# Late heads: where VectorE's pair part and GpSimd's lookup of four PEER heads stand in a streaming-encoder layer

## What is computed

```python
h  = rms_norm(x, g_mix);  z = h @ w_in     # pool 512 | q 512 | k 128 | v 128 | gates 2 x 1024
x  = x + (sigmoid(gate_pool) * (pool_mixer(z_pool) @ w_branch_pool)
          + sigmoid(gate_attn) * (window_attention(q, k, v) @ w_branch_attn)) @ w_out
# PEER: 8 heads, 128 x 128 experts of one neuron, 16 of them per token and head
q  = (rms_norm(x, g_ffn) @ w_q).reshape(T, 8, 256)
s1 = q[..., :128] @ keys_1.T;  s2 = q[..., 128:] @ keys_2.T
v1, i1 = top_k(s1, 16);  v2, i2 = top_k(s2, 16)
vals, ci = top_k(v1[:, None] + v2[None, :], 16)            # over 16 x 16 pairs
e_idx = i1[ci // 16] * 128 + i2[ci % 16];  gates = softmax(vals)
y  = sum over the 128 chosen experts of gates * gelu(h . down[e]) * up[e]
out = rms_norm(x + y, g_final)
```

## Time and profile before

| | us |
|---|---|
| median of 3 runs | 3118.31 (3114.42 to 3119.14) |
| profiled execution, its own time | 3124.53 |
| its span | 3122.7 |
| busy: TensorE | 2829.1 (91%) |
| busy: VectorE | 2353.9 (75%) |
| busy: GpSimd | 2132.2 (68%) |
| busy: ScalarE | 928.8 (30%) |
| mixer, group 0: first xT2 transpose | 342.7 |
| mixer, group 1: first xT transpose | 467.9 |
| mixer, group 1: first branch product | 675.8 |
| gate table: first transpose | 1057.8 |

### The profile page before, as it was taken

How to read it: one execution, slowest core, us unless ns; L and a number is a source line. 1 busy time by engine, 2 the same in 40 slices (tenths; PEclk the granted TensorE clock), 3 DMA queues, 4 the chain that set the end, 5 groups by cost and what they waited for, 6 DMA issues and landing times.

```text
span 3122.7 us, 40081 instructions
## 1 busy us (share of the span) xinstructions
PE 2829.1 (91%) x15235; PEld 2474.5 (79%) x15235; DVE 2353.9 (75%) x4404; ACT 928.8 (30%) x1229; POOL 2132.2 (68%) x1553
## 2 busy tenths in 40 slices
PE   7999888599892399599999999999999999999996
PEld 6688767378781388589989998999899989998995
DVE  2322499532289699398998998889899888989898
ACT  4232432132430399222222222222222222222221
POOL 5334576724366698478877877788777878887774
PEclk9899998699996699799999999999999999999998
DMA  4022421112320188988899998999889989898986
GB/s 144 32 75 95 156 72 50 34 48 96 128 68 0 53 237 228 319 329 328 322 329 328 327 332 298 327 331 329 309 327 327 328 299 332 326 328 311 330 323 222
DMA packets 268048, 716.48 MB, mean 229 GB/s; under 512 B 20496, under 2 KB 106256, under 8 KB 267728
## 3 DMA queue, kind: packets, MB, share of 16 engines
q0 software_dynamic: 111152, 404.54, 34.8%
q1 hardware_dynamic: 156704, 309.38, 29.8%
HBM read 657.47 MB, written 56.36 MB: 229 GB/s over the span
## 4 chain that ended last, share of the span: by engine, by line
PE 41%; DVE 6%; DMA 5%; POOL 4%; issue 2%; ACT 1%; DVEq 0%; SPq 0%; ACTq 0%
PE abank L1427 7%; PE abank L1429 7%; PE abank L1428 7%; PE ybank L1443 7%; PE ybank L1444 7%; PE ybank L1445 7%; DMA up<-in_down,e_idx 3%; POOL up L1377 2%; DVE up L1565 2%; DVE acc L1580 2%; POOL tdown_lo L1382 1%; DMA up<-in_up,e_idx 1%; DVE y L1627 1%; DVE w L1616 1%; POOL tup_lo L1386 0%
## 5 line engine op out<-in xcount | busy, mean ns | idle before, releaser
L1427 PE MATMUL abank<-h2T_hi,tdown_hi 128*128 128x320 f32 x2048 | 635.0, 310 | 40.0 <-DVE h2T_lo L1631 30.7
L1429 PE MATMUL abank<-h2T_hi,tdown_lo 128*128 128x320 f32 x2048 | 635.5, 310 | 0.0
L1428 PE MATMUL abank<-h2T_lo,tdown_hi 128*128 128x320 f32 x2048 | 635.1, 310 | 0.0
L748 POOL TENSOR_TENSOR m_wlo<-m_raw,m_whi 128x1024 fp32r<-128x1024 f32 x116 | 280.3, 2421 | 412.9 <-ACT m_whi L573 411.2
L1580 DVE SCALAR_TENSOR_TENSOR acc<-up,e_act,acc 128x1024 f32<-128x1024 f32 x381 | 489.8, 1286 | 87.8 <-DMA up<-in_up,e_idx 70.3
L1565 DVE CUSTOM_DVE_ANT_0 up<-up,acc 128x1024 f32<-128x1024 f32 x384 | 458.8, 1216 | 109.7 <-DMA up<-in_down,e_idx 98.7
L1443 PE MATMUL ybank<-tup_hi,w_hi 128*128 128x512 f32 x1280 | 504.6, 394 | 19.1 <-DVE y L1627 17.8
L1444 PE MATMUL ybank<-tup_lo,w_hi 128*128 128x512 f32 x1280 | 503.6, 393 | 0.0
L1445 PE MATMUL ybank<-tup_hi,w_lo 128*128 128x512 f32 x1280 | 500.4, 391 | 0.0
L1377 POOL DMA_INDIRECT up<-in_down,e_idx x384 | 405.8, 1057 | 97.9 <-issue 82.1
L1377 POOL DMA_INDIRECT up<-in_up,e_idx x384 | 400.2, 1042 | 103.3 <-issue 89.5
(11 more groups left out here) (206 smaller groups left out, 4662.8 us busy)
## 6 DMA issues: line engine op xcount, KB each, us to landing
tdown<-in_downT SPq DMA_DIRECT2D x128, 512.0 KB
tup<-in_up SPq DMA_DIRECT2D x128, 512.0 KB
m_raw<-in_tiles SPq DMA_DIRECT2D x116, 512.0 KB, 3.3
all_table<-t_out SPq DMA_DIRECT2D x10, 4096.0 KB, 16.4
gates<-all_table SPq DMA_DIRECT2D x64, 640.0 KB
up<-in_down,e_idx POOLq DMA_INDIRECT x384
up<-in_up,e_idx POOLq DMA_INDIRECT x384
m_x<-in_x SPq DMA_DIRECT2D x8, 512.0 KB, 5.3
```

The source lines that it names most:

```text
L1427: nc.tensor.matmul(out, tdown_hi[:, q, at], h2T_hi[:, k, ts], start=k == 0, stop=False)
L1428: nc.tensor.matmul(out, tdown_hi[:, q, at], h2T_lo[:, k, ts], start=False, stop=False)
L1429: ins = nc.tensor.matmul(out, tdown_lo[:, q, at], h2T_hi[:, k, ts], start=False, stop=k == KD - 1)
```

## The change

Four heads of group 0 (4 to 7) are split. Their key part stays where it was and writes tiles of its own (vlate, ilate, in the space of g_ffn). Their pair part stands on VectorE behind m_lo of m = 1, 3, 5, 7 in group 1's merge, the softmax of group 0's gates behind the last of them, and ScalarE's Exp behind out3. GpSimd's lookup is called in halves i = 0, 1: for heads 4 to 6 one half per m from m = 2 on, between the low halves of ga and b of m + 1 (the second half of head 6 at m = 7, behind b7); head 7's behind the low halves of out2 and out5. `keep_choice(0)` goes behind pq2. The order of low halves and pool means in group 1 becomes that of group 0. In all sixteen heads the whole key part now comes before the pair sums, which one set of three instructions makes for all four tiles. The NDOT code goes. Cut to the core:

```diff
+LATE = {1: 4, 3: 5, 5: 6, 7: 7}
+FIRST_LATE = min(LATE.values())
...
-        vtop = place("vtop", [P, 2, 2, TOPK])
+        vtop = place("vtop", [P, TT, 2, TOPK])
-        cand = place("cand", [P, 2, NCAND])
-        cmask = place("cmask", [P, 2, NCAND])
+        cand = place("cand", [P, TT, NCAND])
+        cmask = place("cmask", [P, TT, NCAND])
...
+        vlate = [place(f"vlate{i}", [P, TT, 2, TOPK], F32, at_gffn + 512 * i) for i in range(4)]
+        ilate = [place(f"ilate{i}", [P, 2, TT, TOPK], U32, at_gffn + 2048 + 512 * i) for i in range(4)]
+        hits_late = [hits[0], place("hits_late", [P, TT * TOPK, TOPK], F32, at_pT)]
...
+            def gates_exp(g):
+                act.wait_ge(garg_ready, g + 1)
+                nc.scalar.activation(gate[:], gate[:], ACT.Exp).then_inc(gexp_ready, 1)
...
                 for j in range(4):
-                    if g and j == 1:
-                        act.wait_ge(garg_ready, g)
-                        nc.scalar.activation(gate[:], gate[:], ACT.Exp).then_inc(gexp_ready, 1)
                     keep_raw(g, 1 + j, "q", j)
...
                 for k in range(KD - 1):
                     after("out", k)
+                    if g and k == 3:
+                        gates_exp(g - 1)
...
-            def choose(g, hd):
+            def choose(g, hd, i):
...
-                for i in range(2):
-                    pool.wait_ge(hit_ready, g * 2 * PH + 2 * hd + i + 1)
+                of = hits if g + 1 == NG or hd < FIRST_LATE else hits_late
+                pool.wait_ge(hit_ready, g * 2 * PH + 2 * hd + i + 1)
...
+                if i == 0:
+                    return
...
+                through("q", 0)
                 pool.wait_ge(rope_in, 16 * (g + 1))
-                if g == 0:
...
+                pool_mean(g, 0)
+                through("q", 2)
+                pool_mean(g, 1)
+                through("gp", 0)
+                pool_mean(g, 2)
+                through("ga", 0)
+                pool_mean(g, 3)
                 through("b", 0)
                 for m in range(KD):
                     if 2 <= m + 1 < KD:
                         through("ga", m + 1)
-                    if g:
-                        gather_rows(dots_until(("merge", m - 1) if m else ("tile", 3, 1)) + TT)
+                    if g and m >= 2:
+                        choose(g - 1, FIRST_LATE + (m - 2) // 2, m % 2)
                     if m + 1 < KD:
                         through("b", m + 1)
...
+                if g:
+                    through("out", 2)
+                    choose(g - 1, PH - 1, 0)
+                    through("out", 5)
+                    choose(g - 1, PH - 1, 1)
                 through("pq", 2)
...
+                else:
+                    keep_choice(g - 1)
                 through("pq", 8)
-                for hd in range(PH):
-                    if hd < 3:
-                        tile_low(first + TILE["pq", 8] + 1 + 3 * hd)
-                    else:
-
-                        tile_low(first + NTILE + (3, 4, 7, 10, 10)[hd - 3])
-                    choose(g, hd)
+                for hd in range(PH if g + 1 == NG else FIRST_LATE):
+                    tile_low(first + min(NTILE + 3, TILE["pq", 8] + 1 + 3 * hd))
+                    for i in range(2):
+                        choose(g, hd, i)
...
+            def top_keys(g, hd, values, places):
+
+                dve.wait_ge(ss_ready, g * 2 * PH + 2 * hd + 2)
+                for ts in ((0, 1), (2, 3)):
+                    top16([(s12[hd // 2][:, hd % 2, i, t], smask[:, 2 * (t % 2) + i], values[:, t, i], places[:, i, t])
+                           for t in ts for i in range(2)])
+
+            def top_pairs(g, hd, values, places, to):
+
+                cols = slice(hd * TOPK, (hd + 1) * TOPK)
+                a, b = values[:, :, 0], values[:, :, 1]
+                last = NCAND - HALF_ROW
+                mark(nc.vector.tensor_tensor(cand[:, :, 0:TOPK], a[:, :, 0:1].to_broadcast([P, TT, TOPK]), b, ALU.add))
+                mark(nc.vector.tensor_tensor(
+                    cand[:, :, TOPK:last].rearrange("p t (i j) -> p t i j", j=HALF_ROW),
+                    a[:, :, 1:HALF_ROW].unsqueeze(3).to_broadcast([P, TT, HALF_ROW - 1, HALF_ROW]),
+                    b[:, :, 0:HALF_ROW].unsqueeze(2).to_broadcast([P, TT, HALF_ROW - 1, HALF_ROW]), ALU.add))
+                mark(nc.vector.tensor_tensor(cand[:, :, last:], a[:, :, HALF_ROW:],
+                                             b[:, :, 0:1].to_broadcast([P, TT, HALF_ROW]), ALU.add))
+                linked()
+                top16([(cand[:, t], cmask[:, t], gate[:, t, cols], ctop[:, t]) for t in range(TT)])
...
                     nc.vector.tensor_tensor(mlo[:, m], sg[:, m % 2, 0], mhi[:, m].bitcast(F32), ALU.subtract).then_inc(m_low, 1)
+                    if g and m in LATE:
+                        if m == min(LATE):
+                            dve.wait_ge(pooled_ready, (g + 1) * NPOOL)
+                        i = LATE[m] - FIRST_LATE
+                        top_pairs(g - 1, LATE[m], vlate[i], ilate[i], hits_late)
+                if g:
+                    gates_of(g - 1)
...
+                    if more and hd >= FIRST_LATE:
+                        top_keys(g, hd, vlate[hd - FIRST_LATE], ilate[hd - FIRST_LATE])
+                    else:
+                        top_keys(g, hd, vtop, itop)
+                        top_pairs(g, hd, vtop, itop, hits)
+            gates_of(NG - 1)
```

More of the change, by code:

```diff
@@ L70 @@
 EARLY = [("gp", 0), ("ga", 0), ("gp", 1), ("ga", 1)]
-NDOT = 0
-DOTS_AT = {("tile", 1, 0): 2, ("tile", 1, 1): 2, ("tile", 2, 0): 2, ("tile", 2, 1): 2, ("tile", 3, 0): 2,
-           ("tile", 3, 1): 2, ("merge", 0): 4, ("merge", 1): 4, ("merge", 2): 8, ("merge", 3): 8, ("merge", 4): 8,
-           ("merge", 5): 8, ("merge", 6): 8, ("merge", 7): 4}
-def dots_until(place):
-    places = list(DOTS_AT)
-    return min(NDOT, sum(DOTS_AT[q] for q in places[:places.index(place) + 1]))
+LATE = {1: 4, 3: 5, 5: 6, 7: 7}
+FIRST_LATE = min(LATE.values())
 def mixer_jobs():
@@ L144, in mixer @@
         wgrp = place("wgrp", [P, NPOOL, P])
+        at_gffn = here()
         gffn = place("gffn", [P, D])
@@ L155, in mixer @@
         hT = place("hT", [P, KD, TT, P], F32R)
+        at_pT = here()
         pT = place("pT", [P, NPOOL, PAD + TG])
@@ L352, in _ @@
                 for i in range(NTILE):
-                    if g and NDOT and i == TILE["out", 3]:
-                        sp.wait_ge(dot_done, NDOT)
-                        load_x(g)
                     if i == TILE["pq", 2]:
@@ L727, in _ @@
                     turned(g + 1, 0)
-            act.wait_ge(garg_ready, NG)
-            nc.scalar.activation(gate[:], gate[:], ACT.Exp).then_inc(gexp_ready, 1)
-            if NDOT:
-                act.wait_ge(dot_done, NDOT)
-                nc.scalar.activation(dots[:, 0:NDOT], dots[:, 0:NDOT], ACT.Gelu_apprx_tanh).then_inc(act_ready, 1)
+            gates_exp(NG - 1)
         @block.gpsimd
         def _(pool):
-            own, made, gathered = [0], [0], [0]
+            own, made = [0], [0]
             def link(ins):
@@ L878, in _ @@
         def _(dve):
-            own, dots_made = [0], [0]
+            own = [0]
             def link(ins):
@@ L914, in turned_low @@
                                                in1=hT[:, k].bitcast(F32), op0=ALU.mult, op1=ALU.subtract).then_inc(hT_low, 1)
-            def some_dots(g, *place):
-                to = dots_until(place) if g and place in DOTS_AT else 0
-                while dots_made[0] < to:
-                    c = dots_made[0]
-                    dve.wait_ge(down_in[c % TT], 16 * (c // TT + 1))
-                    if c == 0:
-                        dve.wait_ge(h2_in, 16)
-                    row = x[:, c % TT]
-                    nc.vector.tensor_tensor_reduce(out=row, in0=row, in1=gffn[:], scale=1.0, scalar=0.0, op0=ALU.mult,
-                                                   op1=ALU.add, accum_out=dots[:, c:c + 1]).then_inc(dot_done, 1)
-                    dots_made[0] += 1
+            between = []
@@ new lines, in top16, with step @@
+            def top16(chains):
+                def step(op, first):
+                    if between:
+                        between.pop(0)()
+                    for c, (scores, masked, values, places) in enumerate(chains):
+                        if not first:
+                            dve.wait_ge(dve_own, done[c])
+                        mark(op(scores, masked, values, places))
+                        done[c] = own[0]
+                done = [0] * len(chains)
+                step(lambda s, m, v, p: nc.vector.max(v[:, 0:8], s), True)
+                step(lambda s, m, v, p: nc.vector.match_replace(m, v[:, 0:8], s, NEG_BIG), False)
+                step(lambda s, m, v, p: nc.vector.max(v[:, 8:16], m), False)
+                step(lambda s, m, v, p: nc.vector.max_index(p[:, 0:8], v[:, 0:8], s), True)
```

(12 more changed lines are left out.)

195 lines of the change are left out of this document (54 added, 141 removed).

## The result

Nine executions each: before 3116.87 us (3114.39 to 3124.99), after **3099.57 us** (3094.11 to 3109.93). The ratio is 0.9944, interval 0.9936 to 0.9953: 17.3 us less, faster by 0.56%, a small gain but clear of the noise. The prediction was 3108, its range 3091 to 3118. The profiled execution after took 3103.28 us (span 3101.5), 21.2 us less than the profiled one before.

A forecast was written before the change was run, and what follows sets the result against it. VectorE's backlog on group 0's last heads was taken to delay group 1's front, and VectorE to bound the tail. Terms -39.5 + 23.7 + 8.7 - 3 = -10.1 us from the median 3118.3 gave 3108 us, range 3091 to 3118.

The forecast's parts named there:

- Front: Group 1 up to the merge: scores at 549.0 instead of 586.79, scores to merge 1.7 us shorter; -39.5 us.
- The template: Group 0's front without backlog: 46.22 us from last pool tile's copy to scores, 87.35 from there to first branch matmul.
- Cover of the front: Group 1's rope, first product wanted at 519.8: some 5 us of slack for VectorE, beyond which rope starts later.
- rope starting after 525: Group 1's front: named as a sign that the prediction is wrong.
- Rival 4: Front misses template as last four heads' keys outlast 519.8 by 6 us; 3114 us, within Rival 2's chance of 0.12.
- Merge: Group 1's merge: three pauses of 5.2 us before b3, b5, b7, each with 2.7 of lost clock; +23.7 us.
- Out tiles: Behind the merge: 0.9 us before out0, a pause of 5.1 before out3 and 2.7 of clock; +8.7 us.
- Tail: Group 1's heads: 2.4 us from three sums fewer per head, 0.5 from port waits; -3 us.
- Table to end: Stretch from the gate table to the end: no difference expected, 0 us.
- Rival 1: Merge pauses of 5.2 us come without clock loss and the out tiles fit in; 3091 us, chance 0.15.
- Rival 2: Port waits take the front's side gains, pq15's low half 2 to 4 us later, no tail gain; 3114 us, chance 0.12.
- Rival 3: Pair parts in the merge meet GpSimd's low halves, each of three pauses grows by 9.6 us; 3137 us, chance 0.08.

The follow-up runs named there:

- experiment i: On d, all eight heads of group 0 get their old form back; 3106.65 us, ratio 0.9962 to the kernel before.
- k: g with head 4's pair part and lookup back in place and the low halves of tensors k and v ahead of that lookup; 3067.95 us.
- c: Changed kernel with halves undone: whole lookups of heads 4 to 6 at m = 2, 4, 6, ahead of b(m+1)'s low half; 3120.86 us.
- h: Changed kernel, but group 1's pair sums are again two sets of three instructions over two tiles each, new order kept; 3100.07 us.
- e: Changed kernel with the old form of the heads back in group 1 alone; 3105.36 us.
- a: Changed kernel with VectorE's late pair parts ahead of the wait for m_hi and m_lo instead of behind m_lo; 3080.79 us.
- d: Changed kernel with no late head: pair parts and lookups of heads 4 to 7 back ahead of group 1's rope; 3104.97 us.
- g: a plus head 6's second lookup half behind out0's low half and head 7's first half behind out3's; 3069.81 us, ratio 0.9843 to before.
- b: Changed kernel with each lookup half in the merge behind b(m+1)'s low half instead of ahead, head 7's unmoved; 3080.01 us.

## Why the prediction was right, and where it was off

**The mechanism held.** The earlier scores, the pauses, their number and their cause came as forecast. The sum of the terms, -10.1, stands against -21.2 in the profiled executions and -17.3 in the medians; the 7 us by which the forecast gain was too small in the medians come mostly from the front.

**Front, -39.5 expected, -44.0 at b0.** The template was exact: from the last pool tile's copy to the scores 46.21 us (46.22 forecast), from there to b0 87.17 (87.35). The mis-sized step is its start: "Group 1's last pool tile is copied at 502.80" took that copy as fixed. It came 4.3 us earlier, 0.8 by a start that varies and 3.5 by the form of heads 4 to 7, as experiment i shows. The closer low halves, put at "about 1 us" and set against the port, gave 1.2, so that figure was right. What the sum left out is TensorE's clock behind them, 2.3 us: the old kernel ran the tiles there at 0.86, the new one at 1.00.

**Cover of the front.** "If this cover is gone, rope starts that much later; some 5 us of slack are left" was wrong in its size: k spent 13.9 us more and lost nothing that could be read. The sign "rope starting after 525" was wrong with it: in k rope starts at 526.76. Group 0's 60.84 tells when an unhindered VectorE did its first product, not when it was needed. Rival 4 was priced from the same number.

**Merge, +23.7 expected, +22.6 measured.** Hits 6.66 us behind the pair part's start (6.8), lookup 1.31 behind them (1.3), its first half 7.05 long (6.4), pause 5.45 (5.2), three times; clock 2.1 for each (2.7). The second halves cost nothing, as said; c shows what they would have cost in the other place. One sign was named wrongly: it is at even m that VectorE's wait for m_hi shrinks (2.24), at odd m it stays.

**Out tiles, +8.7 expected, +8.8 measured.** 1.06 before out0 (0.9), 5.73 before out3 (5.1), and 2.0 left for the clock (2.7).

**Tail, -3 expected, -4.2 measured.** The single set of sums was put at 2.4 and is 1.4 by h; the port was put at 0.5 and place and order are 2.6 by e and h together, within the spread told there. The sum of the three for four tiles lasts 0.65 us in the merge (658.71 to 659.36), forecast 0.7. The 224-element sum, which the Trainium skill, VectorE: DVE Perf Modes, section on the TRN2 errata, puts at an estimate of 391 ns, took 0.38 us: the trace agrees. The Trainium skill, SBUF — State Buffer, Who interferes with whom, names copy, cast and tensor_scalar beside the instructions with two SBUF inputs as forms that can wait for GpSimd. The trace agrees: casts and tensor_scalar steps of the index work waited like the sums (0.46 to 0.50 us in the mean for 0.19 to 0.23).

**Table to end, 0 expected, -4.5.** No code that issues anything differs there, and the eleven experiments give 2055 to 2062: I take it as spread, the profiled execution before (3124.53) having been 7.7 us above the median. The medians point the same way: the three stretches between the outer columns sum to -16.0, and -17.3 leaves 1.3 us for the rest. More is not shown, since the kernel before has one profile.

**The rivals.** Rival 1 (pauses without loss of clock) fell by the 6.2 us. Rival 2 fell in its sign: the tail gained. Rival 3 (slower) fell, since GpSimd stood waiting for the hits during the exposed part (8.44 us), as argued; what it describes does happen when the pair part comes earlier (2.42 us for a sum in a), but there it is covered.

## What to carry to other kernels

When work moves from a stretch with a backlog into a full one, its place in each queue decides whether anything is gained: behind m_lo the four pair parts gave too little to tell from not moving them (0.9944 against 0.9951 of d), ahead of it, with the lookups behind the tiles, 35 us (3069.8 of g against 3105.0). For another kernel that suggests: look for the engine's longest idle wait in the new stretch (11.6 us here, right before the chosen place) and put the work inside it; on the other queue put the consumer behind the tile that TensorE wants next, and halve it. When a template is used for "needed at", ask whether its event was early or just in time. And when waits of a busy TensorE get shorter, ask for the clock behind them as well as for the waits.

## What the runs showed of the chip

The loss of clock behind a pause did not follow its length. There was none behind 3.25 us; the granted clock was 0.71 in the stretch behind 1.98 us (a), 0.78 in the 7.7 us behind 3.07 us (after, at 935.03), 0.64 behind 3.88 us (a) and behind 8.55 (b), 0.78 behind 5.45 (2.1 us lost), and 0.75 behind 12.00 with hardly more lost. In an out tile, the seventh row of L389 begins 4.2 us behind the first at full clock, but 5.8 us behind a pause of 1.98 us, 5.9 behind 5.73, 6.8 behind 3.88 and 8.55, and 7.1 behind 4.70 (c). So each pause from 5.45 us on cost its length and 1.7 to 2.6 us more here; of the shorter ones some cost clock and some did not.

VectorE's waits beside GpSimd were not those of instructions with two inputs alone: the cast at 892.77 took 2.43 us and ended 0.1 us behind GpSimd's low half, where the same cast takes 0.22 in e.
